# Moving the admission of prompt tiles 5 to 7 behind the barrier, and beginning ScalarE's bisection rounds one unit later, in a hybrid attention and MoE step

## What is computed

```python
def indexer_select(qi, wi, ki, qpos, kpos, topk):
    s = jnp.einsum('bthd,bsd->bths', qi, ki, ...) * (IDX_DIM ** -0.5)
    score = jnp.einsum('bths,bth->bts', jax.nn.relu(s), wi.astype(jnp.float32))
    score = jnp.where(kpos[None, None, :] <= qpos[None, :, None], score, -jnp.inf)
    _, sel = lax.top_k(score, topk)
    valid = sel <= qpos[None, :, None]
    return sel, valid
```

## Time and profile before

| | us |
|---|---|
| median of three runs | 1157.05 |
| lowest, highest | 1151.5, 1157.98 |
| the profiled execution | 1157.81 |
| its span, first to last instruction | 1156.0 |
| TensorE busy | 1061.8 (92%) |
| VectorE busy | 570.6 (49%) |
| ScalarE busy | 412.9 (36%) |
| GpSimd busy | 241.7 (21%) |

### The profile page before, as it was taken

One profiled execution on the slowest core, in us unless ns is written; L12 is line 12 of the kernel. 1 busy time (PEld: TensorE's weight loads), 2 busy tenths in 40 slices (PEclk: granted clock), 3 DMA queues, 4 the chain that ended last, 5 costly groups with the idle time before them and its releaser, 6 DMA issues. The chain is left out here.

```text
span 1156.0 us, 16386 instructions
## 1 busy us (share of the span) xinstructions
PE 1061.8 (92%) x6188; PEld 721.7 (62%) x6188; DVE 570.6 (49%) x1275; ACT 412.9 (36%) x975; POOL 241.7 (21%) x298
## 2 busy tenths in 40 slices
PE   6999989999997999999997998799999999999980
PEld 3643334444454777777785565487878787878860
DVE  4406699999987866666846551314111111111114
ACT  2325534878454545455631333211111111111114
POOL 4741116643411000000004210011212121212110
PEclk9999989999995999999998899799999999999995
DMA  8600000010192311111011761599999999999928
GB/s 267 227 20 1 1 18 1 1 42 0 38 231 85 130 45 47 43 51 55 20 56 64 292 232 67 201 379 337 326 337 343 335 344 333 343 334 342 285 31 320
DMA packets 51342, 191.42 MB, mean 166 GB/s; under 512 B 10926, under 2 KB 13950, under 8 KB 41029
## 3 DMA queue, kind: packets, MB, share of 16 engines
q1 hardware_dynamic: 39583, 142.71, 34.8%
q0 software_dynamic: 11536, 47.71, 14.6%
q10 hardware_dynamic: 158, 0.16, 0.1%
HBM read 162.49 MB, written 28.19 MB: 165 GB/s over the span
## 5 line engine op out<-in xcount | busy, mean ns | idle before, releaser
L1562 PEld LDWEIGHTS ps<-mem 128*128 128x128 f32 x2048 | 236.5, 194 | 16.8 <-issue 16.8
L1562 PE MATMUL ps<-mem 128*128 128x96 f32 x2048 | 235.9, 277 | 0.8 <-DVE mem L2577 0.8
L1638 ACT ACTIVATE mem<-ps 128x512 f32<-128x512 f32 (+7 forms) x340 | 150.1, 480 | 229.2 <-PE ps L1355 62.1
L2136 DVE TENSOR_SCALAR_CACHE_REDUCE mem<-mem 128x768 bf16<-128x768 f32 (+2 forms) x134 | 166.5, 1286 | 0.0
L1403 PE MATMUL ps<-mem 128*128 128x256 f32 x512 | 118.3, 384 | 1.9 <-DVE mem L2425 1.1
L1568 PE MATMUL ps<-mem 128*96 128x512 f32 x256 | 117.6, 602 | 2.5 <-DVE mem L2569 2.5
L2569 DVE TENSOR_TENSOR mem<-mem,ps 128x192 f32<-128x192 f32 x32 | 11.4, 355 | 212.8 <-ACT mem L2012 212.8
L1022 POOL DMA_INDIRECT h_rows<-mem x32 | 46.5, 1454 | 295.9 <-DVE mem L2584 295.9
L1403 PEld LDWEIGHTS ps<-mem 128*128 128x128 f32 x512 | 95.8, 192 | 15.9 <-DVE mem L2441 2.4
L2012 ACT ACTIVATE mem<-ps 128x192 f32<-128x192 f32 x32 | 10.6, 332 | 262.5 <-PE ps L1562 262.5
L1568 PEld LDWEIGHTS ps<-mem 128*96 128x96 f32 x256 | 39.0, 162 | 57.1 <-issue 51.2
(11 more groups left out here) (308 smaller groups left out, 1460.7 us busy)
## 6 DMA issues: line engine op xcount, KB each, us to landing
mem<-in_expert_w_gate SPq DMA_DIRECT2D x32, 1024.0 KB
mem<-in_expert_w_up SPq DMA_DIRECT2D x32, 1024.0 KB
mem<-in_expert_w_down SPq DMA_DIRECT2D x32, 1024.0 KB
mem<-in_x_prompt SPq DMA_DIRECT2D x16, 512.0 KB, 4.2
mem<-in_w_in SPq DMA_DIRECT2D x3, 2048.0 KB, 10.8
h_rows<-mem SPq DMA_DIRECT2D x8, 512.0 KB, 2.6
xn_rows<-mem SPq DMA_DIRECT2D x8, 512.0 KB, 2.9
mem<-h_rows SPq DMA_DIRECT2D x8, 512.0 KB, 5.3
```

The source lines that it names most:

```text
L1562: ins = mm(ps[:, 2 + s, j * CAP:(j + 1) * CAP], wgu[w][:, j // 2, k, (j % 2) * P:(j % 2 + 1) * P], xgT[:, s, k, :], start=(k == 0), stop=( ...
L1638: return fn(out, in_, ACT.Copy, scale=scale)
L2136: v.tensor_scalar(bufs[a % 3][0:R, 0:w], sc, mid[:, a:a + 1], None, ALU.is_ge, ALU.add, accum_out=cnt[:, a:a + 1]).then_inc(step, 1)
```

## The change

Admission of FAR leaves the stretch ahead of the barrier: `admit_group(far, 3)` goes, and `selections()` does the same 18 passes as pieces after NEAR's. The `PIECES` table is rewritten so that all pieces still end in tile 7: tiles 2 and 3 get 2, 2, 2, 3 pieces after their four S in place of 4 each, tile 4 gets 6 each, tiles 5 and 6 get 7 each; tiles 0, 1 and 7 keep theirs. `masks_ready` comes after both groups. On ScalarE, `some_rounds(1)` does nothing, so the rounds start at n = 2.

```diff
-HALVING = {"S": 4}
-PIECES = [[{"S": 2, "V": 1}] * 3 + [{"S": 2, "V": 2}], [{"S": 2}] * 4] + [[HALVING] * 4] * 5
+PIECES = [[{"S": 2, "V": 1}] * 3 + [{"S": 2, "V": 2}], [{"S": 2}] * 4]
+PIECES += [[{"S": 2}] * 3 + [{"S": 3}]] * 2 + [[{"S": 6}] * 4] + [[{"S": 7}] * 4] * 2
 PIECES += [[{"S": 4, "V": 4}] * 3 + [{"S": 1}]]
...
             def some_rounds(n):
-                for _ in range(6):
+                for _ in range(6 if n >= 2 else 0):
                     next(between, None)
...
             halvings(far, 3, ITERS - 4)
-            admit_group(far, 3)
             take_coarse(0)
...
             def selections():
                 unhalve(near, 0)
                 for a in range(3):
                     yield from admit(near[a], a)
+                    tiles_admitted.append(NEAR[a])
+                unhalve(far, 3)
+                for a in range(3):
+                    yield from admit(far[a], 3 + a)
+                    tiles_admitted.append(FAR[a])
                 dve.nop().then_inc(masks_ready, 1)
-                near_admitted.append(True)
```

More of the change, by code:

```diff
@@ L2212, in take_coarse @@
                 link(v.tensor_tensor(mid, lo, hi, ALU.add))
[L2214 to L2217, removed]
             def select(group, c0, step, ready):
@@ L2476, in last_chunk @@
                 return ("T", i, h, g, 4 if i >= 4 else 0)
-            near_admitted = []
+            tiles_admitted = list(range(NEAR[0]))
             def selections():
@@ L2498, in _ @@
                     h, w, u = t[2], P * (i + 1), i * PAIRS + t[2]
-                    assert i < NEAR[0] or near_admitted
+                    assert i in tiles_admitted
                     take(dve, "2b", "A", t)
```

## The result

| | before | after |
|---|---|---|
| median, us | 1157.06 (six runs) | 1186.12 (six runs) |
| lowest, highest | 1151.5, 1158.07 | 1184.94, 1187.36 |
| ratio | | 1.0266, 95% interval 1.0246 to 1.0286 |
| profiled execution, its span | 1157.81, 1156.0 | 1186.04, 1184.1 |

The change makes the kernel 2.7% slower. (A slice of after is 29.6 us long. The 12th and 13th are the stretch around the barrier.)

The account below looks back on a forecast made before the run. TensorE's own work, the gaps in it and the clock lost behind gaps were taken to bound the kernel. 1157.8 - 3.9 (ScalarE) + 20.4 (gaps) + 10.5 (clock) = 1184.8, median 1184 us, range 1170 to 1193.

Parts of the forecast that it names:

- The sign, and bank M: Prompt attention: VectorE's extra pieces stand ahead of the add of OP that frees bank M, so TensorE waits; slower 0.94.
- the rival "faster": Extra pieces lie in VectorE's idle time, bank M is free in time, only ScalarE's 3.9 us tell: 1154; chance 0.03.
- The gaps in the attention: Prompt attention, tiles 1 to 6: TensorE's waits at OT, XR and LG for the add grow by 20.4 us.
- The clock: Prompt attention: six TensorE gaps of 2.5 us or more each cost 1.75 of lowered clock, 10.5 in all.
- The case without clock loss: Rival: gaps in the attention cost their length but the clock stays up, about 1174 us; chance 0.22.
- ScalarE's start at unit 2: Phase 1, unit 1: TensorE's gap and its clock loss go, 4.4 us; phase 2a starts 0.5 later: 3.9 gained.
- Admission ahead of the barrier is free in itself: Before the barrier: removing admission alone gains nothing, as TensorE ends last; it keeps ScalarE's 3.9 us from being cut to 2.0.
- Moved waits, later stages: Behind the attention: `masks_ready` some 60 us later delays GpSimd's first sample-key loads, used near 635, at no cost.

Follow-up runs that it names:

- add_first: Changed kernel with the pieces behind the scores of tiles 2 to 6 moved directly behind the residual add of OP: 1159.29 us, ratio 1.0032.
- spread: Changed kernel with the table of pieces for tiles 1 to 6 set by hand, iteration by iteration, 106 pieces as there: 1148.36 us, ratio 0.9937.
- admit_only: Changed kernel with ScalarE's rounds back at unit 1, so only the moved admission and new table of pieces: 1187.89 us, ratio 1.0291.
- warm_short: Changed kernel with three or two dummy matmul calls ahead of six TensorE waits for bank M, about the gaps' length: 1175.38 us, ratio 1.0171.
- rounds_only: Kernel before with only ScalarE's rounds starting at unit 2, admission staying ahead of the barrier: 1154.41 us, ratio 0.9992.
- warm_gaps: Changed kernel with six or five dummy matmul calls ahead of six TensorE waits for bank M: 1186.44 us, ratio 1.0274.
- halved: Changed kernel with about half of each iteration's pieces behind V instead of behind S, same number per iteration: 1158.73 us, ratio 1.0022.

## Why the prediction was right, and where not

The forecast was 1184 in a range of 1170 to 1193, the time 1186.1. Step by step:

- **The sign, and bank M.** Right, and shown by `add_first`: the same work on VectorE in the same iterations, with the add ahead of it, takes 26 out of the stage. The mean busy share of VectorE, which spoke for the rival "faster", does not tell the two apart: it does the same work here (175.7) and in `spread` (174.3), where TensorE never waits for the add.
- **The gaps in the attention**, 20.4. Measured 20.5 of idle time more. All but one came within 0.3 of their figures, among them XR of (2, 2) 1.48 for 1.3, XR of (3, 2) 2.76 for 2.55, LG 2.85, 2.98 and 2.91 for 2.6, 2.8 and 2.8, OT of (6, 0) 2.58 for 2.5. The exception is OT of (5, 0), 1.78 for 2.5: the clock was still down from the gap ahead of it, so the transposes and OP behind the scores took 5.4 (1.54 + 3.87) in place of 4.5 (0.87 + 3.62) while VectorE went on at its own pace. In `admit_only` the same gap is 2.65.
- **The clock**, 10.5 as six falls of 1.75. Measured 12.3, so the term was 1.8 short, in both of its factors: five gaps were followed by a fall and not six, three cost 1.7 each, as taken, but the two behind LG of (4, 3) and (5, 3) cost 4.9 and 3.4. (One of the two figures behind the 1.75, the 1.86 of the gap at 236.77, was scaled from a group of 16; against the 4.56 that the same ten matmuls take at full speed it is 1.7.) The case without clock loss is refuted by `warm_short`: with the idle time filled and bank M as late as before, 11 come back. The rule of the Trainium skill, "TensorE: Matmul & The Clock Gate", section "HAM oscillation — how this bites in real kernels", which stood behind that case, names only longer idle gaps as a danger; the trace does not agree, with a clock of 0.68 to 0.86 in the stretches behind gaps of 2.58 to 2.98.
- **ScalarE's start at unit 2**, -3.9. Measured -6.0 at the first scores, in these steps: the gap 2.8 and its clock 1.8 (4.4 expected for the two), less 1.0 for a later start of phase 2a (TensorE waits 1.39 for ScalarE at 300.63, where it waited 0.39 before), of which 0.8 came back because the DMA wait near 313 (0.60 in the view of before) is missing here (0.5 expected for the two), and 1.7 from the second gap, at which the clock did not fall in this execution. The last is chance and not the change: `add_first` has the same instructions up to the barrier and shows 6.26 at that place.
- **Admission ahead of the barrier is free in itself** and only keeps ScalarE's gain from being cut to 2.0. Right: 2.0 were cut in `rounds_only` (TensorE's wait 4.35 for 2.35), and in the profile of after VectorE is idle for 11.55 ahead of its copy, where some 12 were forecast.
- **Moved waits, later stages**: right, 108.72 against 108.98. The experts took 1.5 more; over the profiles of all kernels here that last stage takes 446.0 to 448.7 with no relation to the edits, and I take it for scatter; no run tests that.

The sum came out 1.2 low for the profiled execution (1184.8 against 1186.04): +1.8 from the clock, +1.5 from the experts, -2.1 from ScalarE's part. That these nearly cancel is luck; the largest single miss is 2.1.

## What to carry to other kernels

When spare work is slipped into the order of an engine that is half idle, count what stands between its last input and the next instruction that sets a shared buffer free; the short releasing instruction has to come ahead of the filler, or the filler has to be cut to the slack at that place. Here the same 106 pieces cost 33 us or nothing, by the table alone. A long gap of TensorE can cost more than its length: in the changed kernel five gaps, 14.1 together, cost 12.3 more in clock, while six shorter ones (0.75 to 1.78) cost none.

## What the runs showed of the hardware

The clock's answer to one gap is not fixed. The gap of 2.05 or 2.06 at unit 4 stands in nine profiles with the same ten matmuls behind it: they took 6.25 or 6.26 in four (before, `admit_only`, `add_first`, `halved`) and 4.56 in five (after, `rounds_only`, `warm_gaps`, `warm_short`, `spread`); `add_first` and after run the same instructions up to there. In `add_first` (at 492.27) and in `warm_gaps` (at XR of (5, 2)) a gap of 1.95 was followed by a fall, in after the gap of 2.06 was not. The second of these:

```profile
522.73 0.88 PE L1409 MATMUL ps<-mem 128*128 128x128 f32 x4 [1.95 <-DVE mem L2436]
523.40 1.49 PE L1355 MATMUL ps<-mem 128*128 128x128 f32 x6
```

The fall's length is not fixed either: 1.7 were lost behind three gaps of the changed kernel and 4.9 behind one of 2.98. Why the two behind LG of (4, 3) and (5, 3) were longer is open; there the matmuls of LG itself already ran at 1.2 GHz (3.63 and 3.60 for 1.98, at a granted clock of 0.50 and 0.51), while at LG of (3, 3) they did not (1.98, at 1.00) and the clock fell behind them.
